# The fifth mixer's two scans written as one pipeline of steps: distances on TensorE, scores by blocks, masks ahead of the exponential

## What is computed

```python
def mlstm_scan(...):      # 4 heads of 128; gates logi, logf
    b = cumsum(logf); d = where(mask, b[t] - b[s] + logi[s], -inf)
    mt = maximum(b + m, max_s d)
    s = (q k^T) * exp(d - mt)
    h = (s v + exp(b + m - mt) q C) / maximum(|den|, exp(-mt))
def gla_scan(...):        # 4 heads, keys of 64, values of 128; la is a log decay per key channel
    b = cumsum(la)
    A = einsum(q[t], k[s], exp(b[t] - b[s]))   for s <= t
    o = A v + (q * exp(b)) S ;  S = exp(b_last) S + (k * exp(b_last - b))^T v
y = concat(head_rmsnorm(mlstm) * sigmoid(mo), head_rmsnorm(gla) * silu(gg)) @ w_out
```

## Time and profile before

| | |
|---|---|
| median of 3 runs | 3419.43 us (3419.2 to 3424.58) |
| profiled execution: time, span | 3421.47 us, 3419.6 us |
| mean granted clock of PE | 0.907 |
| busy: PE, DVE, ACT, POOL | 2932.4, 1811.9, 1190.7, 117.9 us |
| chain that ended last | PE 72%, DVE 18%, ACT 5%, issue 3%, DMA 1% |

### The profile page before, as it was taken

One profiled execution on the slowest core, in us unless ns is written; L12 is line 12 of the kernel. 1 busy time (PEld: TensorE's weight loads), 2 busy tenths in 40 slices (PEclk: granted clock), 3 DMA queues, 4 the chain that ended last, 5 costly groups with the idle time before them and its releaser, 6 DMA issues.

```text
span 3419.6 us, 63481 instructions
## 1 busy us (share of the span) xinstructions
PE 2932.4 (86%) x27136; PEld 2454.4 (72%) x27136; DVE 1811.9 (53%) x2743; ACT 1190.7 (35%) x1768; POOL 117.9 (3%) x152
## 2 busy tenths in 40 slices
PE   6999999999999989955436999895597999997898
PEld 6977799997779877733325777673254998995786
DVE  4546555554655542167544777434623554555785
ACT  4445554444554432221113323233101433331333
POOL 0000000000000000000000000000000222220000
PEclk9999999999999999866557999997896999998999
DMA  5544345455435434300001233221110000001343
GB/s 210 179 168 174 124 173 179 166 179 177 159 116 185 160 136 169 141 7 1 1 0 50 111 136 149 104 77 49 49 49 19 4 4 16 4 4 65 131 151 111
DMA packets 49913, 349.53 MB, mean 102 GB/s; under 512 B 5793, under 2 KB 5793, under 8 KB 9185
## 3 DMA queue, kind: packets, MB, share of 16 engines
q1 hardware_dynamic: 49248, 343.56, 28.1%
q0 software_dynamic: 384, 1.90, 0.2%
HBM read 344.39 MB, written 1.05 MB: 101 GB/s over the span
## 4 chain that ended last, share of the span: by engine, by line
PE 72%; DVE 18%; ACT 5%; issue 3%; DMA 1%; DVEq 0%; SPq 0%; ACTq 0%
PE psum L165 72%; DVE wide L87 5%; DVE arena L98 3%; DVE ring_low L87 2%; DVE arena L87 2%; DVE wide L115 1%; DVE wide L98 1%; ACT wide L138 1%; DVE wide L102 1%; ACT w_high L144 1%; PE psum L170 1%; ACT arena L140 1%; DMA ring<-in_evt 1%; DVE wide L94 1%; DMA ring<-in_f_gu 0%
## 5 line engine op out<-in xcount | busy, mean ns | idle before, releaser
L87 DVE TENSOR_TENSOR ring_low<-ring,w_high 128x2048 fp32r<-128x2048 f32 (+3 forms) x254 | 560.2, 2206 | 601.0 <-ACT w_high L144 596.3
L144 ACT ACTIVATE w_high<-ring 128x2048 fp32r<-128x2048 f32 (+3 forms) x254 | 468.9, 1846 | 838.4 <-PE psum L165 488.5
L165 PE MATMUL psum<-x_high,w_high 128*128 128x256 f32 (+1 forms) x2040 | 634.0, 311 | 13.5 <-DVE x_low L87 7.2
L165 PE MATMUL psum<-x_high,ring_low 128*128 128x256 f32 (+1 forms) x2040 | 627.0, 307 | 0.0
L165 PE MATMUL psum<-x_low,w_high 128*128 128x256 f32 (+1 forms) x2040 | 626.9, 307 | 0.0
L165 PE MATMUL psum<-wide,ring 64*64 64x64 f32 (+2 forms) x4400 | 412.8, 267 | 75.8 <-DVE wide L98 43.1
L165 PEld LDWEIGHTS psum<-x_high,w_high 128*128 128x128 f32 x2040 | 390.7, 192 | 50.1 <-issue 16.8
L165 PEld LDWEIGHTS psum<-wide,ring 64*64 64x64 f32 (+1 forms) x4400 | 296.2, 146 | 168.7 <-issue 95.1
L165 PEld LDWEIGHTS psum<-x_high,ring_low 128*128 128x128 f32 x2040 | 390.5, 191 | 18.5
L165 PEld LDWEIGHTS psum<-x_low,w_high 128*128 128x128 f32 x2040 | 390.8, 192 | 17.1
L165 PE MATMUL psum<-wide 64*64 64x64 f32 (+1 forms) x6192 | 284.0, 234 | 113.2 <-DVE wide L87 104.5
(11 more groups left out here) (188 smaller groups left out, 3553.6 us busy)
## 6 DMA issues: line engine op xcount, KB each, us to landing
ring<-in_f_gu SPq DMA_DIRECT2D x88, 1024.0 KB, 4.9
ring<-in_w_mod SPq DMA_DIRECT2D x48, 1024.0 KB, 4.9
ring<-in_fu SPq DMA_DIRECT2D x44, 1024.0 KB, 4.8
ring<-in_f_dn SPq DMA_DIRECT2D x40, 1024.0 KB, 4.9
ring<-in_w_in SPq DMA_DIRECT2D x28, 1024.0 KB, 4.9
ring<-in_fd SPq DMA_DIRECT2D x20, 1024.0 KB, 4.8
ring<-in_rkvr SPq DMA_DIRECT2D x12, 1024.0 KB, 4.7
ring<-in_w_out SPq DMA_DIRECT2D x8, 1024.0 KB, 4.9
```

The source lines that it names most:

```text
L87: self.done(self.eng.tensor_tensor(o, a, b, op), then)
L144: self.done(self.eng.activation(o, i, ACT.Copy, scale=scale), then)
L165: ins = self.eng.matmul(o, l, r, start=a, stop=z)
```

## The change

- GLA: the distances of all five levels and of the two state factors come from a matmul of the log decay `LA` with constant matrices (`gw`, `STRICT`, `DIAG`), straight into bank 0; ACT takes the exponential from there. There is one item (unit and kind) per step, 28 in 36 steps; DVE multiplies it one step later and PE makes its scores three steps later, with two buffers each. Scores are made only where they count: blocks of 64, 32, 16 (into a bank first filled by a matmul with zeros, `tile 128x512`), and 32-column blocks for the two finest levels, which alone are masked (`CMT`) and multiplied by the values in 32 by 32 blocks. States of a unit are made in one bank, before they are needed.
- mLSTM: eight stages (head, direction) of four steps. DVE adds a mask of -1e30 to the row gate once per stage (`ED`), ACT adds the column gate as its bias inside the exponential, writing into `MPT`; DVE multiplies by the scores once. The denominators are taken four at a time, and in direction 0 ACT scales the results.
- The gate rows are steps 0 to 3 of the mLSTM generator. Squares, sums and gates of the head norms, and two weight splits, are steps too; the root is applied per head, alternating with `x_low`.
- The constants' load grows from 768 to 1152 columns, and the load that replaces them waits for the end of the mLSTM's masks and of GLA's.

```diff
+            for j, ph in STEPS:
+                if j < 8 and ph == 0:
+                    hd, z, _ = stage_of(j)
+                    T.bank(5, ml_a["off", j])
+                    te.wait_ge(*row_a[z])
                     te.wait_ge(*row_d[z, "neg"])
-                    T.mm(bank(z), ident[0:4, hd:hd + 1].to_broadcast([4, 128]), RM[z][0:4, :], True, True,
-                         ml_mm((hd, "bm", z)))
...
+                    T.mm(bank(5), ident[0:4, hd:hd + 1].to_broadcast([4, 128]), RM[z][0:4, :], True, True, ml_mm(("bm", j)))
+                if 0 < j < 9 and ph < 3:
+                    p = j - 1
+                    hd, z, kbs = stage_of(p)
+                    for n in ((0, 1), (2,), (3,))[ph]:
+                        kb = kbs[n]
+                        lo, hi = span_of(z, kb)
+                        T.bank(6 + n % 2, ml_d["p", p, n])
+                        T.mm(bank(6 + n % 2)[:, lo:hi], q8[:, 4 + hd, 128 * kb:128 * kb + 128], q8[:, hd, lo:hi], True, True,
+                             ml_mm(("q", p, n)))
+                if 0 < j < 9 and ph == 3:
+                    p = j - 1
+                    hd, z, _ = stage_of(p)
...
+                        T.bank(6 + tp, ml_d["y", p] if z else ml_a["y", p])
+                        te.wait_ge(*ml_d["p", p, 3])
...
+            for j, ph in STEPS:
+                if j < 8 and ph == 1:
+                    hd, z, kbs = stage_of(j)
+                    se.wait_ge(*ml_d["e", j])
+                    if j > 1:
+                        se.wait_ge(*ml_mm["v", j - 2, 1])
+                    for kb, lo, hi in (((0, 128, 512), (1, 256, 512), (2, 384, 512)),
+                                       ((1, 0, 128), (1, 256, 512), (0, 256, 512), (3, 256, 384)))[z]:
+                        col = 16 * z + 4 * kb + hd
+                        A.act(MPT[z][:, kb, lo:hi], bank(5)[:, lo:hi], ACT.Exp, ml_a(("off", j)) if kb == 2 + z else None,
+                              bias=gc[:, col:col + 1])
+                if j < 8 and ph == 2:
+                    hd, z, kbs = stage_of(j)
+                    se.wait_ge(*ml_d["e", j])
...
+                        col = 16 * z + 4 * kb + hd
+                        A.act(MPT[z][:, kb, 128 * kb:128 * kb + 128], ED[:, 128 * kb:128 * kb + 128], ACT.Exp,
+                              ml_a(("diag", j)) if kb == kbs[3] else None, bias=gc[:, col:col + 1])
...
+            for j, ph in STEPS:
+                if j < 8 and ph == 0:
+                    ve.wait_ge(*ml_mm["bm", j])
+                    if j:
+                        ve.wait_ge(*ml_a["diag", j - 1])
+                    D.stt(ED.rearrange("p (b t) -> p b t", b=4), bm(STRICT[j % 2], 4), -1e30,
+                          bank(5).rearrange("p (b t) -> p b t", b=4), ALU.mult, ALU.add, ml_d(("e", j)))
+                if 0 < j < 9 and ph < 3:
+                    p = j - 1
+                    hd, z, kbs = stage_of(p)
+                    ve.wait_ge(*ml_a["diag", p])
+                    for n in ((0,), (1,), (2, 3))[ph]:
+                        lo, hi = span_of(z, kbs[n])
+                        ve.wait_ge(*ml_mm["q", p, n])
+                        e = MPT[z][:, kbs[n], lo:hi]
+                        D.stt(e, bank(6 + n % 2)[:, lo:hi], 128 ** -0.5, e, ALU.mult, ALU.mult, ml_d(("p", p, n)))
...
+        def item(i):
+            return i // 14, i // 7 % 2, KIND[i % 7], i // 7
...
         def gla_pe(T):
             te = T.eng
-            for u in UNITS:
-                z, hp = u
-                T.bank(4, gl_d[u, "cum"])
...
+            for t in TICKS:
+                if t < 28:
+                    z, hp, kind, u = item(t)
+                    T.bank(0, gl_d["cl", t] if kind == 0 else gl_a["ex", t])
+                    te.wait_ge(*lsn_ok[0])
+                    w = STRICT[z] if kind == "ek" else DIAG[z] if kind == "eb" else gw[:, z, kind, :]
+                    for c in FOUR:
+                        T.mm(bank(0)[:, 128 * c:128 * c + 128], LA[:, c, 256 * z + 128 * hp:256 * z + 128 * hp + 128], w,
+                             True, True, gl_mm(("dx", t)) if c == 3 else None)
...
+                        te.wait_ge(*gl_a["hi", u, a])
+                        T.bank(3 + a, gl_d["y", u, a] if z else gl_a["y", u])
+                        for n, c in enumerate(chunk_order(z)):
+                            s = slice(128 * c, 128 * c + 128)
+                            T.mm(bank(3 + a)[:, s], GAT[a][:, s], GV[:, c, v0 + 128 * a:v0 + 128 * a + 128], n == 0, False)
+                    for n, c in list(enumerate(chunk_order(z)))[1:]:
...
                         for a in TWO:
                             r = slice(64 * a, 64 * a + 64)
-                            T.mm(bank(gla_banks(lev)[a])[:, s], GKT[r, s], GQT[r, s], True, True,
-                                 gl_mm((u, "at", lev, a)) if c == 3 else None)
...
+                            T.mm(bank(3 + a)[:, s], GQB[r, s], GSS[r, 128 * n - 128:128 * n], False, False,
+                                 gl_mm(("os", u)) if n == 3 and a else None)
...
+                        for c in FOUR:
+                            for g in FOUR:
+                                r = slice(32 * g, 32 * g + 32)
+                                o = 256 * a + 32 * c
+                                T.mm(bank(3 + a)[r, 128 * c:128 * c + 128], CMT[r, o:o + 32],
+                                     GV[r, c, v0 + 128 * a:v0 + 128 * a + 128], False, c == 3,
+                                     gl_mm(("o", u, a)) if c == 3 and g == 3 else None)
+                if 2 < t < 31:
+                    scores(T, t - 3)
...
+        def scores(T, i):
+            te = T.eng
+            z, hp, kind, u = item(i)
+            late, early = (0, 1) if z else (1, 0)
+            q, k = GQT[i % 2], GKT[i % 2]
+            rows = [slice(64 * a, 64 * a + 64) for a in TWO]
...
+            elif kind == 4:
+                for a in TWO:
+                    T.bank(3 + a, gl_a["hi", u, a])
+                    T.mm(bank(3 + a), ident[0:4, 8:9].to_broadcast([4, 128]), cst[0:4, 0:512], True, False)
...
+            if kind > 2:
+                m = 16 << (kind - 2)
+                for c in FOUR:
+                    for p in range(64 // m):
+                        e, l = 2 * m * p + m * early, 128 * c + 2 * m * p + m * late
+                        for a in TWO:
+                            T.mm(bank(3 + a)[e:e + m, l:l + m], k[rows[a], 128 * c + e:128 * c + e + m], q[rows[a], l:l + m],
+                                 False, False, gl_mm(("at", i)) if c == 3 and p == 64 // m - 1 and a else None)
...
+            else:
+                if kind == 0:
+                    T.bank(1, gl_d["cm", u])
+                    T.bank(2, gl_d["cm", u])
+                for c in FOUR:
+                    for g in FOUR:
+                        e = 128 * c + 32 * g
+                        for a in TWO:
+                            o = 128 * kind + 32 * c
+                            T.mm(bank(1 + a)[32 * g:32 * g + 32, o:o + 32], k[rows[a], e:e + 32], q[rows[a], e:e + 32], True, True,
+                                 gl_mm(("at", i)) if c == 3 and g == 3 and a else None)
...
+            for t in TICKS:
+                for u in unit_at(t, 6):
+                    i = t - 1
+                    se.wait_ge(*gl_d["kt", i - 2])
+                    se.wait_ge(*gl_d["cl", i])
+                    A.act(GEX[i % 2], GDX, ACT.Exp, gl_a(("ex", i)), scale=1.0 / 16)
+                    A.act(GDX, GDX, ACT.Exp, gl_a(("ne", i)), scale=-1.0 / 16)
+                if t < 28 and t % 7 != 5:
+                    if t > 1:
+                        se.wait_ge(*gl_d["kt", t - 2])
+                    se.wait_ge(*gl_mm["dx", t])
+                    A.act(GEX[t % 2], bank(0), ACT.Exp, gl_a(("ex", t)), scale=1.0 / 16)
...
+        def decayed(D, i):
+            ve = D.eng
+            z, hp, kind, u = item(i)
+            q, k = GQ[:, hp, :], GQ[:, 2 + hp, :]
+            late, early = (0, 1) if z else (1, 0)
+            ex, qt, kt = GEX[i % 2], GQT[i % 2], GKT[i % 2]
+            ve.wait_ge(*gl_a["ex", i])
...
+            if kind == "ek":
+                D.tt(kt, k, ex, ALU.mult, gl_d(("kt", i)))
+            elif kind == "eb":
...
+            elif kind == 0:
+                ve.wait_ge(*gl_a["ne", i])
+                D.tt(qt, q, ex, ALU.mult)
+                D.tt(kt, k, GDX, ALU.mult, gl_d(("kt", i)))
...
+                for u in unit_at(t, 9):
+                    if u:
+                        ve.wait_ge(*gl_mm["o", u - 1, 1])
+                    ve.wait_ge(*gl_mm["at", 7 * u + 6])
                     for a in TWO:
...
-                        ve.wait_ge(*gl_mm[u, "at", lev, a])
-                        if ago and lev == 0:
-                            ve.wait_ge(*gl_mm[ago, "o", 3, 1])
-                        to = GTM if lev else GAT[a]
-                        D.tt(to.rearrange("p (c j) -> p c j", c=4), bank(gla_banks(lev)[a]).rearrange("p (c j) -> p c j", c=4),
```

(66 more changed lines are left out.)

577 lines of the change are left out of this document (291 added, 286 removed).

## The result

| | before | changed |
|---|---|---|
| median, runs (same chip, taken with the changed kernel's) | 3422.01 us, 4 | 3258.27 us, 4 (3254.83 to 3262.93) |
| profiled execution: time, span | 3421.47, 3419.6 | 3254.83, 3253.0 us |
| busy: PE, DVE, ACT | 2932.4, 1811.9, 1190.7 | 2911.7, 1697.1, 1215.8 us |

The ratio is 0.9522 (95% interval 0.9505 to 0.9540): the kernel is 164 us faster. Forecast were 3306, with a range of 3258 to 3400: the time lies inside the range, 0.3 us above its lower edge, and 22 us under the forecast's own range of 3280 to 3330. Single runs of the changed kernel lie on both sides of that edge. In the profiled executions the difference is 3421.47 - 3254.83 = 166.6 us, and the projection behind the mixer starts 1815.3 - 1648.2 = 167.1 us earlier: all of it comes from this stage.

The account below looks back on a forecast made before the run. The stage was taken as bound by DVE while both scans run, then by GLA's ring. Scans from 1481 plus 187 us PE, 12 waits, 20 tail start the projection at 1700, not 1815.3: 3421.5 - 115 = 3306 us, range 3258 to 3400.

Parts of the forecast that it names:

- rival E: Rival for the scans: full clock throughout and no cost for divisions, 146 + 8 us, giving 3261 us; chance 0.10.
- The ring: GLA level before the change: ACT exponential, DVE multiplies, PE matmuls, DVE mask and add, one at a time; 8.2 us.
- PE's time in the scans, 187 us: PE's work in both scans after 1481, with 70% of the time at 2.4 GHz, mean clock 0.85.
- my own two sums: PE's work in the scans, divisions included: 162 us at 2.4 GHz, 293 us at 1.2 GHz.
- my lower bound of 0.016: GLA score blocks: record cost in proportion to columns, half the 0.032 us taken from 64 by 64 by 64.
- The price of 0.29 per distance: PE price of a 128 by 128 by 128 matmul at 2.4 GHz, from eight records in 1.16 us.
- Divisions, 0.13 at full clock: Array division changes about three times in each of 40 steps: 16 us at full clock, 31 at slow.
- Neither is the bound any more: DVE at 96 us with gaps and ACT at 63 us stop bounding the scans, if steps overlap as written.
- A: Rival: PE stays at 1.2 GHz in the scans because low tiles don't wake it; 3412 us, chance 0.10.
- B: Rival: steps run in lockstep, so PE's 187 and DVE's 96 us add up; 3390 us, chance 0.15.
- C: Rival: array drains at every block, 608 at 0.26 us, and the clock stays slow; 3570 us, chance 0.05.
- D: Rival: masked-score blocks in four row strips writing one bank run one after another, 0.29 us each; 3338 us, chance 0.12.

Follow-up runs that it names:

- run 4: Two kernels from the changed one: every distance matmul issued twice on TensorE, 3276.05 us; every product with the decays made twice on VectorE, 3283.97 us.
- run 3: From the changed kernel, in 20 of 28 steps three distances moved into the score blocks: all together (control), 3268.52 us; one by one, 3291.45 us.
- run 2: Changed kernel with the 128 matmuls of masked scores times values ordered strip by strip instead of alternating the four row strips: 3283.51 us.
- 5: Changed kernel with the mLSTM's 44 steps first and then the 36 of GLA, not both in one pipeline: 3304.78 us.
- run 1: Changed kernel with the 64 block records of levels 0 and 1 issued four times over in each unit, 1536 more records: 3308.78 us.

## Why the prediction was right, and where not

- **The ring goes, and the stage is shorter by what it waited.** Right. Gate rows end at 1479 (1481), ScalarE 64.1 us (63), VectorE 84.1 (96), PE 86% busy (over 85%), mean clock 0.88 (0.85), the tail 20.7 (20).
- **The range.** That the time lies in it is luck: the median is 0.3 us above the lower bound, the profiled run 3.4 below it, and the bound stands only 3 us below rival E's 3261, whose reasons did not come true.
- **PE's time in the scans, 187 us.** This is the term that was mis-sized: 127.3 us, 60 less, where waits were 20 (12). The last values ended at 1627.5, not 1680, and that is the whole difference to the forecast. Its parts, worked out: by my own two sums the slow clock costs 293/162 of the fast, so 127.3 us, with the clock low for 24% of the time, are 114 us of work at full clock, against 162. (a) Score blocks: 960 records by 0.032 are 30.7 us, measured 13.9. The nearest row, 64 by 64 by 64, was too far: a record of 32 columns costs 0.012 (64 in 0.76) and lies under my lower bound of 0.016, but one of 16 columns costs 0.011 (64 in 0.73), over its bound of 0.008, so cost in proportion to the columns is wrong too (0.0145 on average, 0.010 in long runs). (b) The price of 0.29 per distance is a group's whole time through its matmuls: eight records take 1.05 to 1.16, sixteen of the shape 1.95, so that the second eight add 0.8 to 0.9, or 0.20 to 0.22 a matmul; run 4 has groups of sixteen distances, and they take 1.95 to 2.05. What a group costs beyond this is its end and the change to the next, and I added that once more as 16 us of divisions. (c) The 512-column matmuls: four records in 1.77, 0.89 a matmul and not 0.99. That is an argument from rows: how the remaining 31 us split between (b), (c) and other shapes no run separates.
- **Divisions, 0.13 at full clock.** The price was right (0.147 measured), the way of adding it was not.
- **"Neither is the bound any more" (VectorE).** Wrong, as run 4 shows: 27 us more on VectorE cost 26, 11 of 28 in the trace as waits of PE and the rest as a lower clock. The forecast of what it does on PE's path left out that the buffer for distances is single.
- **A**: not in this kernel; run 3 shows it in one stretch of 24 us. **B**: in part; PE's 127 and VectorE's 84 don't add up (147.5), but more work on either lengthens the stage. **C**: refuted, 64 block records in 0.76. **D**: refuted by rows and by run 2. The Trainium skill's rule on one PSUM bank for different row tiles (TensorEngine Tiling (Array Packing), Gotcha 1) does not show in this shape: four strips, each with partitions of its own in one bank, take 0.030 us per record when they alternate and 0.067 when one strip follows the other. The same page's overhead of 60 cycles per matmul is not seen either: it would be 0.025 us at 2.4 GHz, as an estimate from that page, and 64 records start in 0.76 us, 0.012 each.
- **E**: 3261, the time nearest to the 3258 measured, but not by its reasons: the clock was 0.88 and changes cost. Two errors of mine, blocks and groups, made the sum come out there.

## What to carry to other kernels

A group's duration divided by its count is no unit price: take the difference between a long and a short group, and charge a change of tile shape once. Before calling an engine hidden, look at the largest lump of its work against the buffers ahead of it, not at its share of busy time. When tiles of different shapes alternate, collect them in groups: the change costs 0.15 us at full clock, and in one stretch of 24 us fine alternation went with a clock of 0.50 on a full engine. And before a cost is put down to waits or to work, compare busy time and clock of the unchanged instructions: in runs 2, 4 (VectorE's work) and 5 a large part of what an edit cost in the trace (12 of 27, 17 of 28 and 29 of 47 us) was the clock of matmuls that it had not touched.

## What had not been expected of the hardware

- Small block matmuls in eight tiles start 0.010 to 0.012 us apart, but not without end: in run 1 PE stood ten times, 1.0 to 2.5 us each, for "issue", nine times after 109 to 256 in a row and once after 33 that stood 2 us behind a group of 93. At what length this begins no run here fixes.
- Row strips of 32, one after another, take 0.067 us a record, alternating 0.030 (run 2). In the first of the two stretches shown there PE was 4.00 of 4 us busy and the clock stayed at 0.50.
